# Order of a two-mixer transformer kernel: paired half units behind scores and turns, scalings ahead of outputs, order around both mixers

## What is computed

```python
def first_block(x, ...):
    x = x + 0.5 * swiglu(rmsnorm(x, norm_ffn1), w_ffn1_gate, w_ffn1_up, w_ffn1_down)
    x = x + hybrid_mixer(rmsnorm(x, norm_mix), w_in, ..., w_out, rel_bias)
    x = x + 0.5 * swiglu(rmsnorm(x, norm_ffn2), w_ffn2_gate, w_ffn2_up, w_ffn2_down)
    return rmsnorm(x, norm_final)

def hybrid_mixer(h, w_in, ...):
    qa, ka, va, qb, kcb, vcb, ksb, vsb, kwb, vwb, gb = split(h @ w_in)
    out_a = moba_attention(qa, ka, va, ...)     # 8 heads, one block of 256: causal attention with bias
    out_b = nsa_attention(qb, ...)              # 8 heads, 2 key groups: compressed keys (an MLP over 32
                                                # tokens), selected blocks and window, each with a gate
    return concat(out_a, out_b) @ w_out

def second mixer:                               # differential attention (4 heads, 2 softmaxes each)
    o_da = diff_attention(...)                  # and a gated linear recurrence in both directions
    o_hg = hgrn2_bidirectional(...)
    x = x + concat(o_da, o_hg) @ w_out
```

## Time and profile before

| | |
|---|---|
| median of 3 runs | 883.4 us (883.01 to 883.76) |
| profiled execution | 884.17 us, its span 882.4 us |
| TensorE matmuls busy | 872.1 us (99%), granted clock 0.999 of full speed |
| TensorE weight loads | 730.8 us (83%) |
| VectorE | 649.3 us (74%) |
| ScalarE | 494.6 us (56%) |
| GpSimd | 134.8 us (15%) |
| first mixer | about 199 to 334 us of the span |
| second mixer | about 515 to 655 us |

### The profile page before, as it was taken

One profiled execution on the slowest core, in us unless ns is written; L12 is line 12 of the kernel. 1 busy time (PEld: TensorE's weight loads), 2 busy tenths in 40 slices (PEclk: granted clock), 3 DMA queues, 4 the chain that ended last, 5 costly groups with the idle time before them and its releaser, 6 DMA issues.

```text
span 882.4 us, 15426 instructions
## 1 busy us (share of the span) xinstructions
PE 872.1 (99%) x5304; PEld 730.8 (83%) x5304; DVE 649.3 (74%) x1004; ACT 494.6 (56%) x771; POOL 134.8 (15%) x117
## 2 busy tenths in 40 slices
PE   9999999999999999999999999999999999999997
PEld 6888888888677778888888978877888888888986
DVE  6766666666689876766666668899766878878785
ACT  6554454447466657445445466567747545545566
POOL 2241101001000002100100021640002221221130
PEclk9999999999999999999999999999999999999999
DMA  9786666555654354666656537553266665665521
GB/s 302 248 277 205 190 226 202 170 156 167 190 181 137 116 166 140 198 204 198 190 182 199 187 105 237 162 165 100 74 193 201 192 191 190 188 192 191 184 79 48
DMA packets 122285, 157.13 MB, mean 178 GB/s; under 512 B 10079, under 2 KB 83555, under 8 KB 122240
## 3 DMA queue, kind: packets, MB, share of 16 engines
q1 hardware_dynamic: 119888, 151.67, 54.3%
q0 software_dynamic: 1760, 4.28, 1.8%
q10 hardware_dynamic: 592, 0.59, 0.2%
HBM read 155.43 MB, written 1.07 MB: 177 GB/s over the span
## 4 chain that ended last, share of the span: by engine, by line
PE 93%; DVE 4%; ACT 2%; issue 1%; DMA 0%; ACTq 0%; DVEq 0%
PE bank L610 22%; PE bank L562 16%; PE bank L564 15%; PE bank L563 15%; PE bank L612 12%; PE bank L595 1%; PE bank L594 1%; PE bank L593 1%; PE bank L885 1%; PE bank L1111 1%; PE bank L1087 1%; PE bank L1099 1%; PE bank L1207 0%; PE bank L972 0%; PE bank L1246 0%
## 5 line engine op out<-in xcount | busy, mean ns | idle before, releaser
L2094 DVE TENSOR_TENSOR w_lo<-w_raw,w_hi 128x1024 fp32r<-128x1024 f32 x179 | 244.2, 1366 | 111.9 <-ACT w_hi L1451 110.7
L1451 ACT ACTIVATE w_hi<-w_raw 128x1024 fp32r<-128x1024 f32 x180 | 190.6, 1059 | 167.1 <-PE bank L564 74.1
L610 PE MATMUL bank<-x_hi_lo,w_hi 128*128 128x512 f32 x864 | 211.2, 391 | 0.0
L610 PEld LDWEIGHTS bank<-x_hi_lo,w_hi 128*128 128x128 f32 x864 | 158.5, 188 | 30.7 <-DVE arena L2296 0.3
L562 PE MATMUL bank<-w_hi,x_hi_lo 128*128 128x512 f32 (+3 forms) x376 | 151.5, 403 | 0.5 <-DVE arena L2518 0.5
L2087 DVE TENSOR_TENSOR w_lo<-w_raw,w_hi 128x1024 fp32r<-128x1024 f32 x95 | 116.9, 1250 | 40.3 <-ACT w_hi L1442 39.9
L564 PE MATMUL bank<-w_hi,x_hi_lo 128*128 128x512 f32 (+3 forms) x376 | 144.2, 384 | 0.0
L563 PE MATMUL bank<-w_lo,x_hi_lo 128*128 128x512 f32 (+3 forms) x376 | 144.0, 383 | 0.0
L1442 ACT ACTIVATE w_hi<-w_raw 128x1024 fp32r<-128x1024 f32 x96 | 99.2, 1055 | 41.0 <-PE bank L564 33.5
L612 PEld LDWEIGHTS bank<-x_hi_lo,w_lo 128*128 128x128 f32 x864 | 110.9, 191 | 4.9 <-issue 0.6
L612 PE MATMUL bank<-x_hi_lo,w_lo 128*128 128x256 f32 x864 | 112.6, 283 | 0.0
(11 more groups left out here) (340 smaller groups left out, 972.1 us busy)
## 6 DMA issues: line engine op xcount, KB each, us to landing
w_raw<-in_w_ffn_down SPq DMA_DIRECT2D x132, 256.0 KB, 3.3
w_raw<-in_w_ffn_gate SPq DMA_DIRECT2D x131, 256.0 KB, 2.9
w_raw<-in_w_ffn_up SPq DMA_DIRECT2D x131, 256.0 KB, 3.1
w_raw<-in_w_in SPq DMA_DIRECT2D x104, 256.0 KB, 3.2
w_raw<-in_w_out SPq DMA_DIRECT2D x32, 256.0 KB, 3.4
w_raw<-in_w_ple_gate SPq DMA_DIRECT2D x16, 256.0 KB, 3.3
arena<-bias_rows POOLq DMA_DIRECT2D x8, 256.0 KB, 5.0
w_raw<-in_cmp_w_k SPq DMA_DIRECT2D x8, 256.0 KB, 4.0
```

Source lines behind the costliest of these rows:

```text
L610: mm = pe.matmul(o[:, :], wh[:, kk, c], xhl_k, start=k == 0, stop=k == 7)
L1451: act.activation(whi[:, slot * UNIT:(slot + 1) * UNIT], raw[:, slot * UNIT:(slot + 1) * UNIT], ACT.Copy).then_inc(sem("hi_done"), 1)
L2094: dve.tensor_tensor(wlo[:, s_], raw[:, s_], whi[:, s_].bitcast(F32), ALU.subtract).then_inc(sem("lo_done"), 1)
```

## The change

- TensorE, first mixer: an even step is now scores, turns, beside; then the half units of both steps of the pair come together (those of the even step, then those of the odd one), then pv and the odd step's beside. hid_turn(1) goes from the end of step 6 to step 7 ahead of pv.
- VectorE: in an odd step the scalings come ahead of o_out, then the staging of a projection, beside, and the splits of units. In an even step beside comes first, as before. The copy of the compressed keys (kcmp_done) comes behind the scalings. cmp_softmax goes from step 3 to step 2. KA0's split goes from step 2 to step 3.
- ORDER: CK3 comes ahead of QA1, hid_unit(0, 3) ahead of the third half unit. The splits around it follow.
- ScalarE counts its stagings in `pj_act`, VectorE in `pj_done`; a first half unit of tile 0 waits for ScalarE's alone, one of tile 1 for VectorE's alone.
- FILL_AT: step 8 has two half units in place of one, step 14 one in place of two.
- Behind the loop VectorE's last split of three goes behind norm_x.
- Second mixer: VectorE does the two splits that GpSimd did, in steps (3, 2) and (3, 3); da_scores(1) comes ahead of level 15; ScalarE's weights_turned(2) comes behind the staging of projection 7.

```diff
 U_QB = U_KC + 4
-ORDER = "QB0 QB1 QB2 CK0 QB3 CK1 QA0 CK2 QA1 CK3 QA2 QA3 CV0 CV1 KA0 CV2 CV3 KA1 KA2 KA3".split()
+ORDER = "QB0 QB1 QB2 CK0 QB3 CK1 QA0 CK2 CK3 QA1 QA2 QA3 CV0 CV1 KA0 CV2 CV3 KA1 KA2 KA3".split()
...
-        STG_AFTER = [2, 4, 4, 4, 6, 6, 8, 8, 10, 10]
+        STG_AFTER = [1, 2, 2, 2, 3, 3, 4, 4, 5, 5]
...
-        POOLED = (U_IN2 + 20, U_IN2 + 21)
-
-        def pooled(u):
-            return sum(w < u for w in POOLED)
-
         def lo_ready(u):
...
-            if u - 1 in POOLED:
-                return sem("lo_pool"), pooled(u)
-            return sem("lo_done"), u - whole(u) - pooled(u)
+            return sem("lo_done"), u - whole(u)
...
         def lo_shift(base):
-            return whole(base) + pooled(base)
-
-        FILL_AT = (0, 1, 2, 3, 4, 5, 6, 7, 8, 9, 9, 10, 11, 12, 13, 14, 14, 15, 16, 17)
+            return whole(base)
+
+        FILL_AT = (0, 1, 2, 3, 4, 5, 6, 7, 8, 8, 9, 9, 10, 11, 12, 13, 14, 15, 16, 17)
         CV_AT = {3: (0, 1), 5: (2, 3)}
         OUT_AT = ((0, 0, 18), (0, 1, 19), (1, 0, 20), (1, 1, 21), (3, 0, 22), (4, 0, 23), (2, 0, 24), (2, 1, 24))
         HI_AT = {3: (U_KA[1],), 5: (U_KA[2], U_KA[3]), 7: (U_VA, U_VA + 1, U_VA + 2), 9: (U_VA + 3, U_OUT1),
                  10: (U_OUT1 + 1,), 12: (U_OUT1 + 2,), 14: (U_OUT1 + 3,), 15: (U_OUT1 + 4,), 17: (U_OUT1 + 5,)}
-        LO_AT = {2: (U_KA[0],), 4: (U_KA[1],), 6: (U_KA[2], U_KA[3]), 8: (U_VA, U_VA + 1), 10: (U_VA + 2, U_VA + 3),
+        LO_AT = {3: (U_KA[0],), 4: (U_KA[1],), 6: (U_KA[2], U_KA[3]), 8: (U_VA, U_VA + 1), 10: (U_VA + 2, U_VA + 3),
                  12: (U_OUT1,), 14: (U_OUT1 + 1,), 16: (U_OUT1 + 2,), 18: (U_OUT1 + 3, U_OUT1 + 4),
                  22: (U_OUT1 + 5, U_OUT1 + 6), 24: (U_OUT1 + 7, U_OUT1 + 8)}
...
+                pe.wait_ge(sem("pj_act"), STG_AFTER[g])
                 pe.wait_ge(sem("pj_done"), STG_AFTER[g])
                 if g >= 2:
...
-            def free01(n):
-
-                pe.wait_ge(sem("pj_done"), 2 * n)
+            def free0(n):
+
+                pe.wait_ge(sem("pj_act"), n)
+
+            def free1(n):
+
+                pe.wait_ge(sem("pj_done"), n)
...
             def hid_unit(s_, j):
...
                 u = U_VA + j if b == 2 else (U_QA, U_KA)[b][j]
-                if j == 0 and m == 0:
-                    free01(3 + b if b else 1)
+                if j == 0:
+                    (free1 if m else free0)(3 + b if b else 1)
                 if m == 0:
                     pe.wait_ge(*lo_ready(u + 1))
...
             tgroup(4, stg_tile)
+            hid_unit(0, 3)
             filler()
             tgroup(5, lambda m, q: stg_tile(m, 2 + q))
             filler()
-            hid_unit(0, 3)
...
             def hid_turn(s_):
...
                 if s_ == 5:
                     tgroup(6, stg_tile)
-                if s_ == 6:
-                    hid_turn(1)
                 if s_ == 7:
                     tgroup(7, lambda m, q: stg_tile(m, 2 + q))
...
                     tgroup(s_ - 4, lambda m, q: stg_tile(m, 2 * (s_ - 12) + q))
             for s_ in range(24 + 2):
-                if s_ < 24 and s_ % 2 == 0:
-                    scores(s_)
+                if s_ % 2 == 0:
+                    if s_ < 24:
+                        scores(s_)
+                    if s_ >= 2:
+                        probs_turn(s_ - 2)
+                        probs_turn(s_ - 1)
+                    beside(s_)
                 for _ in range(FILL_AT.count(s_)):
                     filler()
...
                 if s_ == 25:
                     out_half(3, 1)
+                if s_ == 7:
+                    hid_turn(1)
                 if s_ % 2 and s_ >= 3:
                     pv(s_ - 3)
-                if s_ % 2 == 0 and s_ >= 2:
-                    probs_turn(s_ - 2)
-                    probs_turn(s_ - 1)
-                beside(s_)
+                if s_ % 2:
+                    beside(s_)
             assert not fill
             out_half(4, 1)
...
                         tgroup2(*T2_AT[p, j])
                     for n in LEVELS_AT.get((p, j), ()):
+                        if n == 15:
+                            da_scores(1)
                         level(n)
                     if p >= 6:
...
                             hg_out()
                         if k % 2 == 0:
-                            da_scores(k // 2)
+                            if k != 2:
+                                da_scores(k // 2)
                             if k:
                                 da_turn(k // 2 - 1)
...
                 else:
-                    act.activation(av(STG, [512]), b[:, :], ACT.Copy, scale=r).then_inc(sem("pj_done"), 1)
+                    act.activation(av(STG, [512]), b[:, :], ACT.Copy, scale=r).then_inc(sem("pj_act"), 1)
...
             for p, u in ((0, U_KW), (1, U_KC)):
...
             act.wait_ge(sem("gates_raw"), 2)
             act.activation(sm(GATES, 48), sm(GATES, 48), ACT.Sigmoid).then_inc(sem("gates_done"), 1)
-            split(U_QBS[2] + RING)
+            split(U_CK[0] + RING)
             staged(2, U_QBS[3] + 1)
             split(U_QBS[3] + RING)
...
             filler()
             filler()
-            split(U_QA[0] + RING)
-            filler()
             hid_sums(0)
             filler()
-            split(U_QA[1] + RING)
+            filler()
+            split(U_CK[3] + RING)
...
             def exp(a):
...
                     split(u)
                 for i, m, at in OUT_AT:
-                    if at == s_ and m:
+                    if at + (at + 1) % 2 == s_ and m:
                         split(U_OUT1 + i + RING)
             for i in (3, 4, 5):
...
                     if k == 6:
                         da_exp(3)
-                        weights_turned(2)
                         continue
                     if k == 7:
+                        weights_turned(2)
                         continue
                     if (p, j) not in ((0, 0), (0, 1), (0, 2)):
...
             z(0)
             tg(2)
-            split(U_QBS[2] + RING)
+            split(U_CK[0] + RING)
             tg(3)
             staged(2, U_QBS[3] + 1)
             z(1)
             split(U_QBS[3] + RING)
+            small_values()
             split(U_CK[1] + RING)
-            small_values()
             filler()
             filler()
...
             def beside(s_):
                 if s_ == 1:
-                    hid_silu(0)
                     dve.wait_ge(sem("cmp_full"), 1)
                     dve.tensor_copy(av(KCMP, [30]), bank[2][:, 0:30]).then_inc(sem("kcmp_done"), 1)
-                if s_ == 3:
+                if s_ == 2:
                     cmp_softmax()
                 if s_ == 5:
...
                         if a < 24:
                             ttr(a)
-                beside(s_)
-                for _ in range(FILL_AT.count(s_)):
-                    filler()
-                for u in LO_AT.get(s_, ()):
-                    split(u)
-                if s_ % 2 and 3 <= s_ < 19:
-                    o_out((s_ - 3) // 2)
+                if s_ == 1:
+                    hid_silu(0)
+                if s_ % 2 == 0:
+                    beside(s_)
                 if s_ % 2 and s_ < 24:
                     scale(s_ - 1)
                     scale(s_)
+                if s_ % 2 and 3 <= s_ < 19:
+                    o_out((s_ - 3) // 2)
+                for _ in range(FILL_AT.count(s_)):
+                    filler()
+                if s_ % 2:
+                    beside(s_)
+                for u in LO_AT.get(s_, ()):
+                    split(u)
                 if s_ % 2 and s_ >= 19:
                     pair_lo((s_ - 19) // 2)
...
                                   ).then_inc(sem("nx_ready"), 1)
...
-            for i in (3, 4, 5):
+            for i in (3, 4):
                 split(U_OUT1 + i + RING)
             norm_x(2, R_GAIN + 16, add_out1)
+            split(U_OUT1 + 5 + RING)
             split(U_OUT1 + 6 + RING)
             rstd(2)
...
                         continue
                     if (p, j) == (3, 2):
+                        split(U_IN2 + 4 * p + j + RING)
                         level(2)
                         level(3)
...
                         continue
                     if (p, j) == (3, 3):
+                        split(U_IN2 + 4 * p + j + RING)
                         continue
                     for n in levels:
...
             pool.wait_ge(sem("k_done"), 8)
...
-            def pool_split(u):
-
-                c = slice((u % RING) * UNIT, (u % RING + 1) * UNIT)
-                pool.wait_ge(sem("hi_done"), u + 1 - whole(u))
-                pool.tensor_tensor(wlo[:, c], raw[:, c], whi[:, c].bitcast(F32), ALU.subtract
-                                   ).then_inc(sem("lo_pool"), 1)
-
             def rotate(n, p):
...
                 pool.tensor_tensor(x2, r[2], r[3], ALU.add).then_inc(sem("rot_done"), 1)
...
-            for u in POOLED:
-                pool_split(u)
```

(3 more changed lines are left out.)

6 lines of the change are left out of this document (3 added, 3 removed).

## The result

The changed kernel takes 886.61 us (median of six, 886.12 to 887.12), the kernel before 882.75 (six runs that include the three known, 882.13 to 883.76). The ratio is 1.0044, 95% interval 1.0033 to 1.0054: slower by 3.86 us. The forecast was +4.0 us on 883.4, so 887.4. The sign and the size were right.

What follows compares the result with a forecast made beforehand. TensorE was taken as the bound, 93% of the span. The terms +1.5 + 0.75 + 1.0 + 0.6 + 0.7 + 0.3 - 0.2 + 0.2 - 0.85 = +4.0 us on 883.4 gave 887.4 us, range 882.8 to 889.2.

Steps and rivals of the forecast that it cites:

- opening: Before the first scores: QA1's later load and its split ahead of the staging delay them, +1.5 us (+0.5 to +2.1).
- KA0's split: First KA half unit waits for VectorE's split, moved to the end of step 3: +0.75 us (0.4 to 1.1).
- tgroup(8): Step 12: these transposes wait until cmp_add's first addition empties their bank, +1.0 us (0.7 to 1.2).
- turn of step 20: First mixer: the turn waits for VectorE's pair_lo(0), +0.6 us (0.2 to 0.9).
- turns of steps 24, 22 and 16: First mixer: turns wait for VectorE, step 24 +0.7 us (0.4 to 0.9), 16 and 22 together +0.3 (0 to 0.6).
- steps 6 to 10: Predicted as steps 6 to 9: old gaps of 0.74 us shrink to 0.5 of new waits, -0.2 us (-0.7 to +0.5).
- tile sizes of the new order: TensorE's price for changing tile size, turn instead of half unit behind scores: +0.2 us over twelve pairs (-1.2 to +0.5).
- norm_x: Behind the first mixer: moving OUT1's last split removes the gap ahead of the norm's transposes, -0.35 us.
- second mixer: da_scores(1) ahead of level 15 gains 0.25 us; ScalarE's V staging ahead of weights_turned(2) gains 0.25 us.
- Rivals 1 and 2: Faster: waits don't come, only removals count, 881.1 us, chance 0.13. A wash: half the new waits, 883.4 us, chance 0.17.
- rival 3: Slower still: QA1 lands 0.6 us later and VectorE is late at all twelve turns (+1.2 us), 889.2 us, chance 0.13.
- rival 4: Second mixer loses through VectorE's two more splits, level 4 late: up to +1 us, 888.4 us; chance 0.57 together with the forecast.

Runs made afterwards that it cites:

- x_best3: x_best2 with VectorE's staging of V ahead of the scalings of step 17 and the opening of x_qa1; 878.74 us, ratio 0.9959.
- x_unpaired: x_best3 with every turn and beside of an even step behind the half units; 880.00 us, ratio 0.9968.
- x_qa1: Changed kernel with QA1's split behind the staging of Q on ScalarE, and behind staging and z(1) on VectorE; 885.20 us, ratio 1.0030.
- x_ka0: Changed kernel with VectorE's split of KA0 back in step 2, ahead of the first values' output; 885.55 us, ratio 1.0032.
- x_tg8: Changed kernel with tgroup(8) of step 12 behind the two half units instead of ahead of them; 885.40 us, ratio 1.0027.
- b_pool: Kernel before with only GpSimd's two splits given back to VectorE; 882.54 us, ratio 0.9996.
- x_turns: Changed kernel with TensorE's even steps again scores, half units, turn, small groups; other engines' orders stay changed; 885.20 us, ratio 1.0030.
- x_late: Changed kernel with only the turns of steps 16, 20, 22 and 24 behind their half units; 885.07 us, ratio 1.0030.
- x_best2: x_ka0, x_tg8 and x_late together, old opening, turns of steps 8 and 18 and step 8's value_cmp behind half units, late_lo before step 19's scalings; 881.05 us, ratio 0.9983.

## Why the prediction was right, and where it was not

| step | forecast | measured |
|---|---|---|
| opening | +1.5 | +1.37 |
| KA0's split | +0.75 | +1.07 |
| tgroup(8) | +1.0 | +1.33 |
| turn of step 20 | +0.6 | +0.97 |
| turns of steps 24, 22 and 16 | +0.7 and +0.3 | +1.26 (24 and 22) and +0.50 (16) |
| steps 6 to 10 | -0.2 | -0.35 |
| tile sizes of the new order | +0.2 | -0.90 (0.45 measured at six pairs, the other six taken as alike) |
| key_cmp at step 0, in no row | | -0.18 |
| norm_x | -0.35 | -0.54 |
| second mixer | -0.5 | -0.54 |
| rest, in no row (pairs 18 and 20) | | -0.14 |
| sum | +4.0 | +3.85, by the stages +3.83 |

How the middle rows are measured: a wait is the pair in the changed kernel less the same pair without waits, x_best3 (7.87 less 6.80; 7.61 less 6.28). In steps 8, 16, 18, 20, 22 and 24 the turns of x_best3 are unpaired, so 0.08 is taken off its pair for each: 5.72 and 6.19 less 5.22 (5.30 less 0.08) give 0.50 and 0.97, 9.74 less 8.76 gives 0.98, and 34.60 less 33.34 gives 1.26. The old gaps come from before less x_unpaired: 0.59 (pair 6), 0.74 (pair 10) and 0.54 (the rest). The order is twelve times 0.075, of which only six pairs were compared; step 0 is 0.18. With these, pair 18's 0.03 and 0.17 of before in pair 20 that no bracket shows, the stage comes to 1.07 + 0.98 + 1.33 + 0.50 + 0.03 + 0.97 + 1.26 - 0.59 - 0.74 - 0.54 - 0.17 - 0.90 - 0.18 = +3.02; it was +3.00.

**Right.** The opening, in its mechanism and its landing: ScalarE's split of QA1 starts at 228.33, on its data's arrival, 230.16 on the clock of before (forecast 230.3), and x_qa1 shows that this queue position, on the two engines, is the whole of it (1.70 us). The places and releasers of all the new waits: x_ka0 and x_tg8 remove exactly the named ones. The parts around the mixers: -1.2 together, -0.85 forecast. GpSimd's splits at nothing: b_pool, although VectorE's products shrank by 4.3 us, since TensorE has no gap there. Rivals 1 and 2 are out, for the waits all came. Of rival 3 the late turns came at steps 8, 16, 20, 22 and 24, not at all twelve; rival 4 is out.

**Wrong: the tile sizes of the new order.** The step that failed is "I take +0.2 us over the twelve pairs". The earlier trace rows held 0.20 for a large matmul and 0.15 for four transposes, and the sum of those is -0.05 a pair; I set it aside because no row showed a turn behind scores. The turn costs 0.80, as the prediction said in its last part, and the half unit behind it 0.23. Its own rows would have given -0.6 over twelve pairs; measured is -0.075 a pair, so -0.9. The 0.18 of step 0 is in neither.

**Wrong in size: the waits.** They were forecast at 3.35 from KA0 to the turns, and cost 5.13. Two reasons. First, VectorE's chain was counted short. Changed kernel, chain of waits behind the scores of step 12 and ahead of the turn of step 20:

```profile
281.75 0.91 PE bank L1085 x8
...
283.84 0.61 DVE xg L2631
284.45 0.14 issue
284.58 0.63 PE bank L906 x4
```
```profile
306.10 0.37 DVE x_hi_lo L2688
306.47 0.23 issue
306.70 0.49 DVE x_hi_lo L2696 x2
307.19 0.14 issue
307.32 0.85 PE bank L1097 x6
```

tgroup(8) starts 2.83 us after its scores where I had 2.55; 0.14 of that is the handover back to TensorE, the piece of issue, which was not counted at any wait. The turn of step 20 starts 7.10 after the scores of step 18 (300.22) where I had 6.65: the staging of V does hold the maxima up by 0.3, which I had named and left out, and again 0.14. Second, TensorE's arrival behind a turn was counted too late, 0.86 + 0.80 = 1.66 after the scores. These are pieces of the chain; what a wait delays is the start of the next instruction, and in x_ka0, where it doesn't wait, that start comes 1.48 after the scores (250.54 to 252.02). So the waits of KA0's split and tgroup(8), both behind a turn, were counted 0.18 short. With the 0.14 of the handover that is nearly all of what KA0's split cost beyond the forecast (0.75 forecast, 1.07 measured).

**Wrong in its path: the turn of step 24.** The prediction counts it along VectorE's queue, maxima, splits, scalings and pair_lo. The chain runs through the values just ahead of the turn and ScalarE's pair_hi:

```profile
316.33 0.83 PE bank L1110 x12
...
317.18 0.29 ACT x_hi_lo L1798
...
317.49 0.50 DVE x_hi_lo L2696 x2
...
318.12 0.85 PE bank L1097 x6
```

VectorE's scalings end at 317.41, ScalarE's part at 317.47. A shorter queue on VectorE alone would therefore hardly have shortened this wait: 0.96 us lie between the end of the values (317.16) and the turn.

So +1.8 of missing waits stand against -1.1 of the order, -0.2 at step 0 and -0.3 that the old gaps gave beyond the forecast, and nearly cancel. The forecast that the change is slower rested on sound steps; that it was within 0.2 us on the stages did not.

## What to carry to other kernels

An order on the bottleneck engine is worth its price per pair only as long as the engines that answer it are ahead: here 0.075 us a pair was bought with waits of 0.5 to 1.3 us at five steps. Pair where the answer is ready, leave the cover where it is late, and look for the wait that a wait covers: x_turns, x_late and x_best2 each brought up a new one, and only x_best3 had none. A wait of TensorE can also have no bracket, as key_cmp's 0.18 had none: compare the distances between starts with those of a kernel in which the answer is early. And on an in-order queue a piece that waits for a load belongs behind the pieces that are ready.

## What the hardware showed that I had not expected

- A gap of TensorE costs more than its bracket, by the overlap that is lost, and how much that is depends on what stands ahead of the gap. The first KA product behind its turn, in x_ka0 without a wait and in the changed kernel with one:

```profile
250.54 0.93 PE L1085 MATMUL bank<-arena 64*128 64x128 f32 x8
251.40 0.87 PE L1097 MATMUL bank<-con,arena 128*128 128x128 f32 x6
252.02 0.47 PE L555 MATMUL bank<-w_hi,x_hi_lo 128*128 128x512 f32 x1
```
```profile
251.63 0.87 PE L1097 MATMUL bank<-con,arena 128*128 128x128 f32 x6
253.31 0.47 PE L555 MATMUL bank<-w_hi,x_hi_lo 128*128 128x512 f32 x1 [0.81 <-DVE w_lo L2092]
```

  A turn shows 0.87 us and the product behind it starts after 0.62, so 0.25 of it lies under the product; with the wait it starts after 1.68. The difference is 1.06, the bracket 0.81 and the lost 0.25. Behind a large matmul (0.39 shown, 0.23 to the next start) 0.16 is lost, and the gap of 0.35 ahead of the norm's transposes gave 0.54. Behind scores (0.93 shown, 0.86 to the next start) it is 0.07: 0.93 gave 0.97 and 0.46 gave 0.50. Three more gaps behind turns, with other edits beside them, gave 0.27 (0.47 to 0.74, pair 10), 0.32 (0.27 to 0.59, pair 6) and 0.16 more (1.17 to 1.33, x_tg8, where the group also moved). The Trainium skill has that the end of a TensorE instruction is computed and not observed ("Perfetto Trace Analysis", Tensor Engine Instruction); the overlaps fit that, and no run here tests it.
- VectorE's product of 1024 elements took 3.43 us beside GpSimd's split and 1.21 without it, the one of 512 elements 2.77 and 0.69.
- The first 13 us vary between executions, before any edited instruction: in the fourteen traces of this case the eight transposes shown at the top start between 10.86 (x_late) and 13.04 us (the kernel before). So two profiles of this kernel are compared by distances inside each, not by their spans. Part of it is TensorE's own pace: with the granted clock at 1.00 in both, the second and third large product of the first network show 0.63 us each in the kernel before (at 8.04 and 8.46) and 0.40 in the changed one (at 7.29 and 7.53). Why stays open.
